# Turning the second layer's input by VectorE squares and a DRAM exchange instead of TensorE transposes

## What is computed

```python
def _layer(x, mem, ...):
    (r_q, r_k, r_v, a_cq, a_ckv, a_kpe, l_x, l_v, l_o, l_i, l_f, c_q, z) = _split_cols(x @ w_in, IN_SPLITS)
    # retention, latent attention, mLSTM and memory attention, four heads each;
    # memory attention also needs  k, v = split(mem @ w_mem_kv)
    y = jnp.concatenate([ret, mla, mls, memo], axis=-1) * jax.nn.silu(z)
    y = y @ w_out
    return _layernorm(DEEPNORM_ALPHA * x + y, ln_g, ln_b)

for l in range(DEPTH):
    x = _layer(x, mem, ...)
```

## Time and profile before

| | before |
|---|---|
| median of three runs | 892.65 us (892.63 to 893.07) |
| span of the profiled execution | 891.0 us |
| median less that span | 1.65 us |
| TensorE matmul busy | 884.9 us, 99% |
| VectorE busy | 661.6 us, 74% |
| ScalarE busy | 490.7 us, 55% |
| DMA, mean over the span | 222 GB/s |
| granted TensorE clock | 1.000 |

### The profile page before, as it was taken

The page is one execution under the profiler, slowest core; times in us unless marked ns, Lnnn a source line. Parts: engine busy times, 40 slices in busy tenths (PEclk is TensorE's granted clock), DMA queues, the critical chain, the costliest instruction groups (busy, mean ns, idle before and its releaser), DMA issues.

```text
span 891.0 us, 13209 instructions
## 1 busy us (share of the span) xinstructions
PE 884.9 (99%) x4548; PEld 759.8 (85%) x4548; DVE 661.6 (74%) x1312; ACT 490.7 (55%) x914; POOL 18.0 (2%) x18
## 2 busy tenths in 40 slices
PE   9999999999999999999999999999999999999997
PEld 8888998888888888888888889888888888888896
DVE  6869697877685677766668887968778747689865
ACT  6655775545555346544476556746354653575551
POOL 0000000000000000000000000000000001000001
PEclk9999999999999999999999999999999999999999
DMA  9796498447778687665665966875485865976932
GB/s 358 276 340 201 144 268 271 153 139 226 234 232 287 212 244 254 209 190 191 191 192 187 310 227 171 282 248 158 145 268 177 287 197 154 286 228 230 339 98 94
DMA packets 69650, 198.19 MB, mean 222 GB/s; under 512 B 8136, under 2 KB 21712, under 8 KB 68944
## 3 DMA queue, kind: packets, MB, share of 16 engines
q1 hardware_dynamic: 69008, 196.31, 67.8%
q10 hardware_dynamic: 576, 1.05, 0.4%
HBM read 182.38 MB, written 14.95 MB: 221 GB/s over the span
## 4 chain that ended last, share of the span: by engine, by line
PE 98%; issue 1%; DMA 0%; ACT 0%; POOL 0%; DVE 0%; POOLq 0%; ACTq 0%; DVEq 0%
PE acc L1335 24%; PE acc L1336 24%; PE acc L1339 24%; PE acc L1350 10%; PE acc L1356 5%; PE work L1102 1%; PE work L1101 1%; PE work L1100 1%; PE work L1240 1%; PE work L1239 1%; PE work L1095 1%; DMA B<-in_mem_t 0%; PE work L1262 0%; PE work L1251 0%; PE work L1179 0%
## 5 line engine op out<-in xcount | busy, mean ns | idle before, releaser
L1059 ACT ACTIVATE hi<-raw 128x512 fp32r<-128x512 f32 (+2 forms) x607 | 358.1, 605 | 317.1 <-PE acc L1339 255.5
L1422 DVE TENSOR_TENSOR lo<-raw,hi 128x512 fp32r<-128x512 f32 (+2 forms) x607 | 388.7, 657 | 174.5 <-ACT hi L1059 165.4
L1335 PE MATMUL acc<-hi,xx 128*128 128x512 f32 (+2 forms) x768 | 285.9, 375 | 0.0
L1336 PE MATMUL acc<-hi,xx 128*128 128x512 f32 (+2 forms) x768 | 283.6, 372 | 0.0
L1339 PE MATMUL acc<-lo,xx 128*128 128x512 f32 (+2 forms) x768 | 223.0, 372 | 0.0
L1335 PEld LDWEIGHTS acc<-hi,xx 128*128 128x128 f32 x768 | 144.6, 188 | 23.6
L1336 PEld LDWEIGHTS acc<-hi,xx 128*128 128x128 f32 x768 | 144.7, 188 | 23.5
L1339 PEld LDWEIGHTS acc<-lo,xx 128*128 128x128 f32 x768 | 140.4, 188 | 24.6
L1350 PE MATMUL acc<-xx,hi 128*128 128x512 f32 x384 | 96.1, 392 | 0.0
L1350 PEld LDWEIGHTS acc<-xx,hi 128*128 128x128 f32 x384 | 69.3, 189 | 12.6
L1356 PEld LDWEIGHTS acc<-xx,lo 128*128 128x128 f32 x384 | 52.4, 190 | 3.7
(11 more groups left out here) (348 smaller groups left out, 972.7 us busy)
## 6 DMA issues: line engine op xcount, KB each, us to landing
raw<-in_w SPq DMA_DIRECT2D x263, 512.0 KB, 4.3
B<-turn SPq DMA_DIRECT2D x80, 128.0 KB, 4.5
raw<-in_w SPq DMA_DIRECT2D x26, 256.0 KB, 2.7
turn<-B SPq DMA_DIRECT2D x12, 512.0 KB, 5.8
raw<-in_w SPq DMA_DIRECT2D x16, 328.0 KB, 3.3
turn<-Y SPq DMA_DIRECT2D x8, 512.0 KB, 5.6
Y<-in_wuq SPq DMA_DIRECT2D x2, 1152.0 KB, 8.6
Y<-in_x_t SPq DMA_DIRECT2D x4, 512.0 KB, 8.7
```

The source lines that it names most:

```text
L1059: act.activation(place(l, t, hi), raw[:, s, (t % 2) * w:(t % 2 + 1) * w], ACT.Copy)\
L1335: pe.matmul(o, ah[:, q], hi[:, s, 0:w], start=k == 0, stop=False, skip_group_check=name == "memv")
L1336: pe.matmul(o, al[:, q], hi[:, s, 0:w], start=False, stop=False, skip_group_check=name == "memv")
L1422: dve.tensor_tensor(place(l, t, lo), raw[:, s, (t % 2) * w:(t % 2 + 1) * w], place(l, t, hi).bitcast(F32), ALU.subtract).then_inc(lo_done. ...
```

## The change

- The 8 `xT` steps of TensorE are gone, with their PSUM banks.
- `normalise` stands at slots 8, 8, 9, 10, 11, 11, 12, 13 in place of 8, 9, 11, 12, 14, 15, 17, 18.
- New VectorE steps `square_x` cb = 0 to 3 after slots 10, 12, 13 and 15: each two STREAM_TRANSPOSEs of 128x512, from `X` into B6, B4, B5, B7.
- SP, behind the raw pairs m = 9, 10, 11, 12: writes the four buffers to a DRAM tensor `x_turn`, 512 KB each; behind m = 12, 13, 14, 15: reads them back into `Y`, four DMAs of 128 KB each.
- `x_hi` and `x_lo` read `Y` in place of the PSUM bank, through the view `x_block`. `x_hi` stands at slots 22 to 29, one each; `x_lo` at 23, 25, 27, 28, 30, 32, 33, 35.
- A few semaphores are merged.

```diff
-for _j in range(8):
-    _put(LATER_PE, 18 + _j // 2 * 4, "xT", _j)
...
-    _put(LATER_ACT, 8 + 3 * _j // 2, "normalise", _j)
-    _put(LATER_ACT, 23 + _j // 2 * 4 + _j % 2, "x_hi", _j)
+    _put(LATER_ACT, 8 + 3 * _j // 4, "normalise", _j)
+    _put(LATER_ACT, 22 + _j, "x_hi", _j)
...
+for _cb in range(4):
+    _put(LATER_DVE, (10, 12, 13, 15)[_cb], "square_x", _cb)
 for _j in range(8):
-    _put(LATER_DVE, (24, 26, 28, 30, 32, 34, 37, 38)[_j], "x_lo", _j)
+    _put(LATER_DVE, (23, 25, 27, 28, 30, 32, 33, 35)[_j], "x_lo", _j)
...
+X_OUT_AT = {9: 0, 10: 1, 11: 2, 12: 3}
+X_IN_AT = {12: 0, 13: 1, 14: 2, 15: 3}
...
+        x_squares = [B[i][:, 0:1024] for i in (6, 4, 5, 7)]
+
+        def x_block(j, n):
+
+            return Y[:, j // 2 * 1024:(j // 2 + 1) * 1024]\
+                .rearrange("p (a i j r) -> p j i a r", a=4, i=NT, j=4)[:, j % 2 * 2 + n]
...
-                        if l == 0:
-                            sp.wait_ge(x_lo.sem, x_lo.at(0, 7))
-                        else:
-                            sp.wait_ge(y_lo.sem, y_lo.at(l - 1, 7))
+                        sp.wait_ge(x_lo.sem, x_lo.at(l, 7))
...
+                    if l and m in X_OUT_AT:
+                        cb = X_OUT_AT[m]
+                        sp.wait_ge(x_squared.sem, cb + 1)
+                        sp.dma_start(a["x_turn"][cb], x_squares[cb]).then_inc(x_turn_out[cb].sem, 16)
+                    if l and m in X_IN_AT:
+                        cb = X_IN_AT[m]
+                        sp.wait_ge(x_turn_out[cb].sem, 16)
+                        if cb == 0:
+                            sp.wait_ge(y_lo.sem, y_lo.at(l - 1, 7))
+                        for b in range(4):
+                            sp.dma_start(Y[b * 32:(b + 1) * 32, cb * 1024:(cb + 1) * 1024].rearrange("c (a n) -> c a n", a=4),
+                                         a["x_turn"][cb, :, b * 256:(b + 1) * 256].rearrange("(a c) n -> c a n", a=4))\
+                              .then_inc(xT_in[cb].sem, 16)
...
-                    wait_job(act, l, ("xT", j))
+                    act.wait_ge(xT_in[j // 2].sem, 16 + 4 * 16)
...
+                def square_x(cb):
+                    dve.wait_ge(normed.sem, 2 * cb + 2)
+                    to = x_squares[cb].rearrange("p (b i j r) -> p i j b r", b=4, i=NT, j=4)
+                    for i in range(NT):
+                        m = dve.transpose(to[:, i], X[:, i, cb * 512:(cb + 1) * 512].rearrange("p (j b c) -> p j b c", j=4, b=4))
+                    m.then_inc(x_squared.sem, 1)
```

More of the change, by code:

```diff
@@ L492, in build_trunk @@
         angles, tables = signal("angles", 0), signal("tables", 0)
-        filled, ready = signal("filled", 0), signal("ready", 0)
+        ready = signal("ready", 0)
         cols_in = signal("cols_in", 1, step=16)
@@ L534, in build_trunk @@
         scaled, copied = signal("scaled", 0), signal("copied", 0)
-        first_gain = signal("first_gain", 0)
+        x_squared, x_turn_out = signal("x_squared", 0), [signal(f"x_turn_out{cb}", 0, step=16) for cb in range(4)]
         stored = signal("stored", 0, step=16)
@@ L781, in _ @@
         def _(pool):
-            pool.wait_ge(ready.sem, 1)
+            pool.wait_ge(ready.sem, 2)
             def root(dst, src, n):
@@ L811, in _ @@
                 load_mem(act, q)
-            act.wait_ge(ready.sem, 1)
+            act.wait_ge(ready.sem, 2)
             act.activation(warm[:, :], half[:, 0:1], ACT.Copy)
@@ L851, in x_hi_ @@
                         return
-                    wait_job(act, l, ("xT", j))
+                    act.wait_ge(xT_in[j // 2].sem, 16 + 4 * 16)
                     act.wait_ge(cols_in.sem, cols_in.at(l, 0))
                     for k in (2 * j, 2 * j + 1):
-                        m = act.activation(xh[:, k, :], bank(l, ("xT", j))[:, (k % 2) * 256:(k % 2 + 1) * 256], ACT.Identity,
+                        m = act.activation(xh[:, k, :].rearrange("p (i a r) -> p i a r", i=NT, a=4), x_block(j, k % 2), ACT.Identity,
                                            scale=cols[:, C_LNG + k:C_LNG + k + 1], bias=cols[:, C_LNB + k:C_LNB + k + 1])
@@ L1081, in _ @@
             pe.sem_inc(tile_used.sem, RING)
-            pe.wait_ge(filled.sem, 1)
+            pe.wait_ge(ready.sem, 1)
             for _ in range(9):
@@ L1105, in both @@
                     return tuple(at(x) for x in parts)
[L1107 to L1115, removed]
                 def mem_scores(h):
@@ L1233, in mla_scores @@
                         pe.wait_ge(rotary_turned.sem, rotary_turned.at(l, 1))
-                        pe.wait_ge(kr_zero.sem, 1)
+                        pe.wait_ge(ready.sem, 3)
                         stand_alone(pe)
@@ L1275, in ret_out @@
                     m.then_inc(job_done.sem, 1)
-                steps = {"xT": xT, "mem_scores": mem_scores, "mem_out": mem_out,
+                steps = {"mem_scores": mem_scores, "mem_out": mem_out,
                          "ml_fold": ml_fold, "ml_q": ml_q, "gateT": gateT,
@@ L1389, in _ @@
             for b in range(BY_MATMUL):
-                pe.wait_ge(gained.sem, b + 1)
+                pe.wait_ge(gained.sem, b + 3)
                 pe.matmul(A_out3(b), tmp[:, 0:P], X[:, 1, b * 512:(b + 1) * 512], start=False, stop=True)\
@@ L1396, in _ @@
         def _(dve):
-            dve.memset(tmp[:, 0:P], 1.0).then_inc(filled.sem, 1)
+            dve.memset(tmp[:, 0:P], 1.0).then_inc(ready.sem, 1)
             dve.memset(half[:, :], -0.5).then_inc(ready.sem, 1)
             dve.memset(krT[ROT:P, 0, :], 0.0)
-            dve.memset(krT[0:ROT, 1, :], 0.0).then_inc(kr_zero.sem, 1)
+            dve.memset(krT[0:ROT, 1, :], 0.0).then_inc(ready.sem, 1)
             for p in range(2):
@@ L1473, in x_lo_ @@
                         for k in (2 * j, 2 * j + 1):
-                            m = dve.tensor_scalar(tmp[:, (k % 2) * 256:(k % 2 + 1) * 256],
-                                                  bank(l, ("xT", j))[:, (k % 2) * 256:(k % 2 + 1) * 256],
+                            m = dve.tensor_scalar(tmp[:, (k % 2) * 256:(k % 2 + 1) * 256].rearrange("p (i a r) -> p i a r", i=NT, a=4),
+                                                  x_block(j, k % 2),
                                                   cols[:, C_LNG + k:C_LNG + k + 1], cols[:, C_LNB + k:C_LNB + k + 1],
                                                   ALU.mult, ALU.add)
-                        m.then_inc(free_bank(l, "xT", j), 1)
-                        wait_read(dve, l, ("xT", j))
+                        link(m)
                         src = tmp[:, :].rearrange("p (k t) -> p k t", k=2)
@@ L1887, in residual @@
                     return m
-                steps = {"angles": angles_, "lo": lo_of, "x_lo": x_lo_, "m_lo": m_lo, "gain": gain, "offset": offset, "kept_lo": kept_lo_, "y_lo": y_lo_, "memv": memv, "mem_max": mem_max, "mem_norm": mem_norm,
+                steps = {"angles": angles_, "lo": lo_of, "x_lo": x_lo_, "m_lo": m_lo, "square_x": square_x, "gain": gain, "offset": offset, "kept_lo": kept_lo_, "y_lo": y_lo_, "memv": memv, "mem_max": mem_max, "mem_norm": mem_norm,
                          "mem_out": out_pair("mem_out", memo), "conv": conv, "rms": rms_, "ckv": ckv, "cqn": cqn_,
@@ L1941, in _ @@
                     for n in (w, 0):
-                        scale(n).then_inc(first_gain.sem, 1)
-                    dve.wait_ge(first_gain.sem, 2)
+                        scale(n).then_inc(gained.sem, 1)
+                    dve.wait_ge(gained.sem, 2)
                     dve.wait_ge(ln_pow.sem, ln_pow.at(l, i))
```

10 lines of the change are left out of this document (4 added, 6 removed).

## The result

The changed kernel takes 897.34 us (median of 6, 896.06 to 900.65), the kernel before 892.69 beside it (median of 6, 892.50 to 893.18): a ratio of 1.0059, 95% interval 1.0049 to 1.0068. It is slower by 4.7 us going by the medians and by 5.3 going by the ratio, which takes in all runs; either way it lies outside my range. Of the experiments' kernels, one that computes the same and moves the same bytes in another form and at other slots takes 890.02.

What follows compares the result with a forecast made beforehand. TensorE was taken to bound the kernel, busy 884.9 of 891.0 us. The sum -3.5 + 1.5 + 0.7 = -1.3 us gave a span of 889.7, or 891.35 beside the median of 892.65; range 889.0 to 895.7.

Steps and rivals of the forecast that it cites:

- 3.5 us off TensorE: Second layer, slots 18 to 32: removing four groups of eight transposes, 0.89 us each, saves TensorE 3.5 us.
- Slots 8 to 17 cost nothing: The added ScalarE and VectorE work there is covered by their reserve; only SP's pair 12 goes out later, at 462.1.
- The rate, 310 GB/s taken, bounds 250 and 350: DMA queue from 463.7: 5.24 MB at 310 GB/s end 1.5 us late; 250 gives 5.6 late, 350 none.
- my own rule: Read 3 must land by 479.1 for slot 29, which needs 340 GB/s; below that it is late.
- The term of 1.5 us in my sum: At the exchange before slot 29: the last read comes 1.5 us late and TensorE waits that long.
- the hidden case: Rival: at 340 GB/s or above the exchange causes no wait, and the kernel takes 889.4 us; chance 22%.
- Lateness one to one: Below 340 GB/s, lateness of the reads passes fully to TensorE, since ScalarE has nothing to catch up with.
- The wait at slot 22, about 4 us, then at 24, 26, 28: Sign on ScalarE: a wait of about 4 us for read 0 at slot 22, then shorter ones at 24, 26, 28.
- `x_hi` from SBUF hardly more than 0.90: ScalarE's x_hi pair takes 0.90 us from PSUM and hardly more when reading Y in SBUF.
- `x_lo` 1.42, VectorE 0.7 more: Slots 28 to 37: x_lo takes 1.42 us, upper bound 1.75, so VectorE without reserve adds 0.7 us.
- After slot 45 the order is as before and the gain is carried along: No further loss after slot 45; the wukv load's wait for x_lo 7, behind pair 22, is free.
- The slower rival: The exchange chokes the weight stream: at 247 GB/s reads come 5.8 us late, giving 895.7 us; chance 20%.

Runs made afterwards that it cites:

- e1: The changed kernel without the exchange's DRAM writes and reads, x_hi and x_lo splitting what already lies in Y, at the same slots: 890.32 us, ratio 0.9972.
- e9: The changed kernel with each 128 KB read taken over 128 partitions and 256 columns in place of 32 partitions and 1024 columns: 894.33 us, ratio 1.0017.
- e5: The changed kernel with x_hi moved to slots 24 to 34 and x_lo to 25 to 37, the exchange at the same places: 894.58 us, ratio 1.0023.
- e6: As e5, with reads 2 and 3 each one raw pair later, behind pairs 15 and 16: 893.53 us, ratio 1.0002.
- e10: The changed kernel with the exchange spread over nine pairs, not seven, each write four DMAs from 32 partitions, each read one over 128: 890.02 us, ratio 0.9966.
- e2: The changed kernel with the reads into 32 partitions bringing each partition's 4 KB in one run instead of four of 1 KB: 898.09 us, ratio 1.0060.
- e11: As e10, but with the writes as in the changed kernel, so Y does not get the transposed input: 890.42 us, ratio 0.9973.

## Why the prediction was wrong

- **3.5 us off TensorE**: right. e1's lx0 at 484.47 against 484.8.
- **Slots 8 to 17 cost nothing; pair 12 at 462.1**: right; 461.37, no wait of TensorE there, and e1 confirms it.
- **The rate, 310 GB/s taken, bounds 250 and 350: the step that failed.** It was 265. With my own rule (needed by 479.1) that is 5.0 us late, and 5.9 were lost; for the 0.9 between them, 0.2 of it from the launch's start, I have no row. The term of 1.5 us in my sum measured 5.9. I had named under 270 as what would make me wrong, and 265 stood in the earlier trace rows; I set it aside because its queue was not always full. That was a misreading: its DMA share is 0.95, and the 301 that I counted as busy has 0.94. And the middle of the three that I called busy is some 320, not 310. I took all stretches of an exchange as one kind and chose their middle. That four reads come in a row here, where there one or two do, I had noted against the hidden case, and I did not carry it to the rate. What the runs showed in its place is the form of the reads: the same bytes into 128 partitions (e9) are 3.0 us faster.
- **Lateness one to one**: incomplete. Besides the rate, ScalarE standing at slot 22 held back the very read that the next `x_hi` needs (SP idle 471.0 to 474.14). I had written the chain down and gave it no price. e5 and e6, the same bytes with later slots, are 2.8 and 3.8 us faster; how much of that is the standing and how much the later need of the reads is not shown. In e9 SP stands as well and the reads are in time, so the standing alone isn't the cause.
- **The wait at slot 22, about 4 us, then at 24, 26, 28**: right in place; 5.00, 1.33, 1.18 and 0.50. TensorE waited before slots 25, 27 and 29, as I had said, and before 23 as well; the waits shrink (1.6, 1.4 and 0.8 from start to start) where I had said that they grow, and I had said 1 to 2 us in all.
- **`x_hi` from SBUF hardly more than 0.90**: 1.00 for a pair (from 471.78 to 472.78).
- **`x_lo` 1.42, VectorE 0.7 more**: VectorE's timeline after has 1.50 from 474.03 to 475.53, and TensorE waited at 499.82, 1.25 us from start to start. The 0.35 that I took for one TENSOR_SCALAR was 0.41. Where no read is late, in e1 and e10, that wait is absent: as the forecast had it, VectorE falls behind only out of the wait.

```profile
474.03 0.73 DVE L1483 TENSOR_SCALAR tmp<-Y,cols 128x256 f32<-128x256 f32 x2
474.80 0.69 DVE L1489 TENSOR_TENSOR xx<-tmp,xx 128x512 fp32r<-128x512 f32 x1
475.53 0.69 DVE L1431 TENSOR_TENSOR lo<-raw,hi 128x512 fp32r<-128x512 f32 x1
```

- **"After slot 45 the order is as before and the gain is carried along"; the `wukv` load free**: wrong, by 2.2 us at 513 and 1.1 at 536 and 816. The wait for `x_lo` 7 was free, as I had it: `x_lo` 7 ended at 496.88, and pair 22 went out behind it at 499.70. But I took pair 22 to come no later than before. It came 3.9 us after the start of lx0 before (492.20), 6.6 in e1 (491.09) and 9.0 in the changed kernel. The 2.7 us in e1, without an exchange, are what the new slots do: `x_lo` 6 and 7, which stood behind `lo` of slot 37 on VectorE, now stand ahead of it, and ScalarE waits 2.02 for `wuq`, TensorE hardly. With the reads late as well, the 1152 KB of `wuq` went out 7.5 us later (500.55 for 493.05), landed after 9.7 us in place of 7.8 and held ScalarE for 4.01.
- **The slower rival** (the exchange chokes the weight stream, 895.7, 20%) was the right mechanism. Its 5.8 us late are the measured 5.9, at a rate of 247 where 265 was measured, and at 265 its own rule gives 5.0, so part of that agreement is luck. It held none of the losses behind slot 45. Against the profiled run (+6.9) it falls 3.9 us short, against the median 1.6.

The sum with measured terms: -3.5 + 5.9 + 1.25 + 2.18 + 0.49 + 0.59 = +6.9, against +6.8 in the profile and +4.7 in the medians. The profiled run is the second slowest of its six (899.64). The changed kernel's runs spread over 4.6 us where those of before spread over 0.7. In single profiles of the experiments ScalarE's wait for wuq goes from 1.21 (e10) to 4.51 (e5), so its landing may be what varies; I did not test it.

## What to carry to other kernels

When work leaves the busy engine by way of a DMA queue, ask what the queue moves in the form that the new transfers have, from a stretch with the same mix, and take the lowest such row as the case to survive, not the middle. Let each DMA into SBUF cover all 128 partitions, and put a rearrangement by groups of 32 on the side that writes DRAM; here that was worth 3.3 us with one set of slots and 1.5 with another. An engine placed to wait for a transfer must not be the one whose progress releases the transfer behind it: spread the pieces so that the first wait falls after its landing.

## What the runs showed of the hardware

With the DMA engines busy throughout, reads from DRAM into 32 partitions each, among 512 KB weight loads, went together with them at 254 GB/s (e2) and 259 (changed) over 468 to 476, and reads over 128 partitions at 359 (e9, also 128 KB each). Run lengths of 1 and 4 KB into the 32 partitions made no difference that shows (897.34 and 898.09 us).

The Trainium skill (SBUF — State Buffer, "Door 1: The DMA port swizzle") states that partitions 0 to 31 reach 8 of 16 ports, so that such a transfer has about half of the rate. The direction agrees with these runs. That the ports are the reason isn't shown: a trace doesn't show them, and no run here has the reads alone in the queue. If reads go at half of 359 and the rest at 359, the 5.24 MB take 8.7 + 11.7 = 20.4 us, an estimate from that page's rule and e9's rate, where 19.8 were measured. For e5 the same sum gives 22.5 us for the 5.98 MB that it moved in 19.8, so what else is in the queue counts too. I had not weighed the rule in the prediction, and by it the choked case would have been the likelier.

The mirror image did not show: with the writes split by 32 partitions the queue moved 392 GB/s over 459 to 468 (e10), against 341 with whole writes (e11), so whether a source in few partitions is slow by itself stays open. A pair of 128x256 instructions on ScalarE took 1.00 us reading `Y` in SBUF in runs of 32 elements and 0.90 reading a PSUM bank; place and runs changed together.
